# Hybrid decoder trunk: squares of x summed through accumulating transposes, the forget-gate chain on ScalarE, and PE matmuls on a constant at the start

## The reference

```python
h = rmsnorm(x, norm_pre[0])                    # x * rsqrt(mean(x*x) + 1e-6) * g
proj = h @ w_in                                # q | k | v | z | f
log_f = log_sigmoid(proj[..., 4096:] + b_f)    # 16 columns, one per head
c = cumsum(log_f)                              # over the tokens
logit[t, s] = q_t . k_s / 8 + c[t] - c[s]      # causal, then softmax
y = (softmax(logit) @ v) * silu(z) @ w_out
x = x + rmsnorm(y, norm_post[0])
x = x + sigmoid(rmsnorm(x, pe_norm[0]) @ pe_w_gate[0]) * (p[0] @ pe_w_proj[0])
```

## Time and profile before

| | |
|---|---|
| median of three runs | 686.02 us |
| profiled execution | 686.55 us, of which 684.7 us span |
| PE busy | 639.0 us (93%) |
| VectorE, ScalarE, GpSimd busy | 417.5, 340.3, 322.1 us |
| mean granted TensorE clock | 0.992 |
| chain that ended last | PE 60%, DVE 17%, issue 10%, ACT 7%, POOL 4% |

### The profile page before, as it was taken

One profiled execution on the slowest core, in us unless ns is written; L12 is line 12 of the kernel. 1 busy time (PEld: TensorE's weight loads), 2 busy tenths in 40 slices (PEclk: granted clock), 3 DMA queues, 4 the chain that ended last, 5 costly groups with the idle time before them and its releaser, 6 DMA issues.

```text
span 684.7 us, 9410 instructions
## 1 busy us (share of the span) xinstructions
PE 639.0 (93%) x2960; PEld 518.2 (76%) x2960; DVE 417.5 (61%) x797; ACT 340.3 (50%) x582; POOL 322.1 (47%) x416
## 2 busy tenths in 40 slices
PE   4979899999999998999979799999999999999697
PEld 2768778787888876788756578888888888887476
DVE  6657786867868786545768853424333343356865
ACT  7746575655656574365537553223231331555452
POOL 6365455646454565000557727564445642003662
PEclk9999999999999999999999989999999999999999
DMA  6233433333333333044002303332223232350032
GB/s 223 94 104 112 121 129 108 100 102 130 114 108 123 121 100 101 32 161 147 0 32 61 123 32 123 123 99 85 92 92 123 92 123 93 103 174 1 31 100 85
DMA packets 27161, 68.69 MB, mean 100 GB/s; under 512 B 3568, under 2 KB 10096, under 8 KB 27136
## 3 DMA queue, kind: packets, MB, share of 16 engines
q1 hardware_dynamic: 27136, 68.37, 30.6%
HBM read 66.23 MB, written 2.13 MB: 100 GB/s over the span
## 4 chain that ended last, share of the span: by engine, by line
PE 60%; DVE 17%; issue 10%; ACT 7%; POOL 4%; DMA 1%; DVEq 0%; SPq 0%; ACTq 0%; POOLq 0%
PE ps_pj L1079 18%; PE ps_pj L1081 17%; PE ps_pj L1080 17%; POOL w_lo L410 3%; PE ps_tr L1088 2%; DVE q_lo L873 2%; DVE act_lo L970 2%; DVE k_st L881 2%; DVE xT L966 1%; DVE t_a L975 1%; ACT logit L527 1%; ACT k_st L573 1%; DVE logit L817 1%; DVE o_u L829 1%; PE ps_tr L1079 1%
## 5 line engine op out<-in xcount | busy, mean ns | idle before, releaser
L410 POOL TENSOR_TENSOR w_lo<-w_raw,w_hi 128x256 fp32r<-128x256 f32 x324 | 259.8, 834 | 134.1 <-ACT w_hi L474 134.0
L1079 PE MATMUL ps_pj<-act_hi,w_hi 128*128 128x512 f32 (+1 forms) x744 | 298.1, 401 | 17.3 <-DVE act_lo L970 10.6
L1081 PE MATMUL ps_pj<-act_hi,w_lo 128*128 128x512 f32 (+1 forms) x744 | 290.6, 391 | 0.0
L1080 PE MATMUL ps_pj<-act_lo,w_hi 128*128 128x512 f32 (+1 forms) x744 | 290.1, 390 | 0.0
L1079 PEld LDWEIGHTS ps_pj<-act_hi,w_hi 128*128 128x128 f32 x744 | 141.1, 190 | 50.5 <-DVE act_lo L970 14.0
L1081 PEld LDWEIGHTS ps_pj<-act_hi,w_lo 128*128 128x128 f32 x744 | 140.7, 189 | 30.0
L1080 PEld LDWEIGHTS ps_pj<-act_lo,w_hi 128*128 128x128 f32 x744 | 141.2, 190 | 24.9
L474 ACT CAST w_hi<-w_raw 128x1024 fp32r<-128x1024 f32 x96 | 99.8, 1047 | 79.5 <-DMA w_raw<-in_weights 66.7
L418 POOL TENSOR_TENSOR bias<-bias,future 128x128 f32<-128x128 f32 x64 | 33.9, 560 | 88.7 <-DMA bias<-negc_scratch 88.7
L527 ACT ACTIVATE logit<-logit,nmax 128x128 f32<-128x128 f32 (+1 forms) x64 | 36.1, 564 | 61.2 <-DVE nmax L808 61.1
L452 POOL TENSOR_TENSOR t_b<-yT,rs 128x512 f32<-128x512 f32 x4 | 7.1, 1770 | 105.2 <-ACT rs L513 105.2
(11 more groups left out here) (143 smaller groups left out, 780.4 us busy)
## 6 DMA issues: line engine op xcount, KB each, us to landing
w_raw<-in_weights SPq DMA_DIRECT2D x100, 512.0 KB, 3.3
bias<-negc_scratch SPq DMA_DIRECT2D x16, 256.0 KB, 7.5
bias<-negc_scratch SPq DMA_DIRECT2D x16, 192.0 KB, 6.3
xT<-in_xT SPq DMA_DIRECT2D x8, 256.0 KB, 5.7
bias<-negc_scratch SPq DMA_DIRECT2D x16, 128.0 KB, 5.0
out<-xT SPq DMA_DIRECT2D x7, 256.0 KB, 3.3
bias<-negc_scratch SPq DMA_DIRECT2D x16, 64.0 KB, 3.4
p_in<-in_pT SPq DMA_DIRECT2D x2, 512.0 KB, 4.6
```

The lines of the kernel that those rows point to most:

```text
L410: last = nc.gpsimd.tensor_tensor(w_lo[place % RING][:, tiles], w_raw[stream(place) % RAW][:, tiles], w_hi[place % RING][:, tiles], ALU.sub ...
L1079: nc.tensor.matmul(out, w_h, a[0][:, k, tokens], start=k == first, stop=False)
L1080: nc.tensor.matmul(out, w_h, a[1][:, k, tokens], start=False, stop=False)
L1081: end = nc.tensor.matmul(out, w_l, a[0][:, k, tokens], start=False, stop=k == last)
```

## The change

In the first stage, ScalarE squares the even tiles and VectorE the odd ones, into four buffers. PE transposes each square in four pieces of 128 x 128, all eight tiles into one PSUM bank with accumulation (`turn_squares`), so that the bank holds the sums over the eight tiles with tokens on the partitions. One reduction on VectorE gives the sum of squares per token, and ScalarE takes its root with the scale 1/1024. `acc` is not made, and `norm_sum(0)` goes. Slot 0 follows two tiles behind instead of three. `norm_spread(0)` moves from the second to the fifth step of slot 1. Twenty matmuls of a constant with itself, 128 columns each, go ahead of everything else on PE.

In the gate chain, the absolute value with the bias moves to ScalarE, min(x, 0) is made together with the bias on VectorE, and the cumulative sum takes both inputs directly; the constant of ones goes. ScalarE's part stands at g = 1 instead of g = 3, and VectorE's sum stands ahead of `scale(1)`. A table with both Exp and Ln is loaded right after the root. Slot 1 is loaded behind x tile 4 instead of 3, and its high part is copied behind tile 5. The bias buffers move to another place in SBUF.

```diff
+WARM = 20
+SQ_BUFS = 4
+SPREAD_AT = 4
...
-BEHIND = 3
+BEHIND = 2
...
-                if k == 1 or k == 3:
-                    load_slot(k // 2, k // 2)
+                if k == 1 or k == 4:
+                    load_slot(k // 3, k // 3)
...
-            sp.wait_ge(f_chain, 3)
+            sp.wait_ge(f_chain, 1)
...
+            nc.scalar.preload_act_table(ACT.Sqrt)
...
-                wait(act, x_acc, k - 1)
-                nc.scalar.activation(sq[k % 2][:], xT[:, k, :], ACT.Square).then_inc(x_sq, 1)
-                if k % 2 == 1 and k < 4:
-                    weight_hi(k // 2, k // 2)
+                if k % 2 == 0:
+                    wait(act, x_turned, k - SQ_BUFS + 1)
+                    nc.scalar.activation(sq[k % SQ_BUFS][:], xT[:, k, :], ACT.Square).then_inc(x_sq[0], 1)
+                if k == 1 or k == 5:
+                    weight_hi(k // 4, k // 4)
...
-            norm_sum(0)
-
             act.wait_ge(f_done, 1)
             nc.scalar.copy(f_half[:], ps_sc[0][F_PART:F_PART + HEADS, :]).then_inc(f_half_done, 1)
-            norm_root(0)
+            act.wait_ge(ssq_done, 1)
+            nc.scalar.activation(root[:], ssq[:], ACT.Sqrt, bias=EPS, scale=1.0 / D).then_inc(root_done, 1)
+            nc.scalar.preload_act_table_set("natural_log_exp_and_others")
             weight_hi(2, 2)
             norm_spread(0)
...
-                    if not attend and g == 3:
-
-                        act.wait_ge(f_chain, 1)
+                    if not attend and g == 1:
+
+                        act.wait_ge(f_scaled, 1)
+                        act.wait_ge(g_loaded[1], 16)
+                        nc.scalar.activation(f_abs[:], f_x[1][:], ACT.Abs, bias=b_f[:]).then_inc(f_act, 1)
+                        act.wait_ge(f_act, 1)
                         nc.scalar.activation(f_ln[:], f_abs[:], ACT.Exp, scale=-1.0).then_inc(f_act, 1)
-                        act.wait_ge(f_act, 1)
+                        act.wait_ge(f_act, 2)
                         nc.scalar.activation(f_ln[:], f_ln[:], ACT.Ln, bias=1.0).then_inc(f_act, 1)
...
-            nc.vector.memset(ones_f[:], 1.0).then_inc(mean_ready, 1)
...
-                dve.wait_ge(x_sq, k + 1)
-                if k == 0:
-                    nc.vector.tensor_copy(acc[:], sq[0][:]).then_inc(x_acc, 1)
-                else:
-                    dve.wait_ge(x_acc, k)
-                    nc.vector.tensor_tensor(acc[:], acc[:], sq[k % 2][:], ALU.add).then_inc(x_acc, 1)
-
-            def f_parts():
-
-                dve.wait_ge(f_half_done, 1)
-                nc.vector.tensor_tensor(f_x[0][:], ps_sc[0][0:HEADS, :], f_half[:], ALU.add).then_inc(f_self, 1)
-
-            norm(0, f_parts)
+                if k % 2 == 1:
+                    wait(dve, x_turned, k - SQ_BUFS + 1)
+                    nc.vector.tensor_tensor(sq[k % SQ_BUFS][:], xT[:, k, :], xT[:, k, :], ALU.mult
+                                            ).then_inc(x_sq[1], 1)
+
+            dve.wait_ge(f_half_done, 1)
+            nc.vector.tensor_tensor(f_x[0][:], ps_sc[0][0:HEADS, :], f_half[:], ALU.add).then_inc(f_sum, 1)
+
+            dve.wait_ge(x_turned, KT)
+            nc.vector.tensor_reduce(ssq[:], ps_tr[0][:].rearrange("p (t c) -> p t c", c=P), AX.X, ALU.add
+                                    ).then_inc(ssq_done, 1)
+            norm_row(0)
...
             def f_logits():
 
-                dve.wait_ge(f_self, 1)
-                nc.vector.tensor_tensor(f_x[1][:], f_x[0][:], rs[0:HEADS, :], ALU.mult).then_inc(f_self, 1)
+                dve.wait_ge(f_sum, 1)
+                nc.vector.tensor_tensor(f_x[1][:], f_x[0][:], rs[0:HEADS, :], ALU.mult).then_inc(f_scaled, 1)
                 dve.wait_ge(g_loaded[1], 16)
-                dve.wait_ge(f_self, 2)
-                nc.vector.tensor_scalar(f_x[0][:], f_x[1][:], b_f[:], None, ALU.add).then_inc(f_self, 1)
-                dve.wait_ge(f_self, 3)
-                nc.vector.scalar_tensor_tensor(f_abs[:], f_x[0][:], -1.0, f_x[0][:], ALU.mult, ALU.max
-                                               ).then_inc(f_chain, 1)
+                dve.wait_ge(f_scaled, 1)
+                nc.vector.tensor_scalar(f_min[:], f_x[1][:], b_f[:], 0.0, ALU.add, ALU.min).then_inc(f_floor, 1)
 
             def f_sums():
 
-                dve.wait_ge(f_act, 2)
-                nc.vector.scalar_tensor_tensor(f_x[1][:], f_x[0][:], 0.0, f_ln[:], ALU.min, ALU.subtract
-                                               ).then_inc(f_chain, 1)
-                dve.wait_ge(mean_ready, 2)
-                dve.wait_ge(f_chain, 2)
-                nc.vector.tensor_tensor_scan(f_negc[:], ones_f[:], f_x[1][:], 0.0, ALU.mult, ALU.subtract
+                dve.wait_ge(f_floor, 1)
+                dve.wait_ge(f_act, 3)
+                nc.vector.tensor_tensor_scan(f_negc[:], f_ln[:], f_min[:], 0.0, ALU.add, ALU.subtract
                                              ).then_inc(f_chain, 1)
 
             def score_logits(u, m0, jj):
@@ -847,8 +850,8 @@
                         scale(0)
                     if g == 4 and not attend:
                         f_logits()
+                        f_sums()
                         scale(1)
-                        f_sums()
...
+            pe.wait_ge(mean_ready, 1)
+            for _ in range(WARM):
+                nc.tensor.matmul(ps_tr[1][:, 0:P], mean_w[:], mean_w[:], start=True, stop=True)
+
+            def turn_squares(k):
+
+                pe.wait_ge(x_sq[k % 2], k // 2 + 1)
+                for t in range(TT):
+                    tokens = slice(t * P, (t + 1) * P)
+                    last = nc.tensor.matmul(ps_tr[0][:, tokens], sq[k % SQ_BUFS][:, tokens], ident[:],
+                                            start=k == 0 and t == 0, stop=k == KT - 1 and t == TT - 1, is_transpose=True)
+                last.then_inc(x_turned, 1)
+
             pe.wait_ge(f_ready, 1)
             for k in range(KT + BEHIND):
+                if 0 < k <= KT:
+                    turn_squares(k - 1)
...
-                if k == KT + BEHIND - 1:
-                    norm_sum(0)
...
-                if k == 1:
+                if k == SPREAD_AT:
...
-                            pe.wait_ge(f_chain, 1)
+                            pe.wait_ge(f_sum, 1)
```

More of the change, by code:

```diff
@@ L25 @@
 ACT = mybir.ActivationFunctionType
+AX = mybir.AxisListType
 P = 128
@@ L148, in trunk @@
         norms = ExitStack()
-        sq = [sb(f"sq{i}", [P, SEQ], at=norms) for i in range(2)]
+        sq = [sb(f"sq{i}", [P, SEQ], at=norms) for i in range(SQ_BUFS)]
         acc = sb("acc", [P, SEQ], at=norms)
@@ L158, in trunk @@
         f_w = sb("f_w", [P, KT, 2 * F_PART], F32R, f_part)
-        ones_f = sb("ones_f", [HEADS, SEQ], at=f_part)
+        ssq = sb("ssq", [P, TT], at=f_part)
+        f_min = sb("f_min", [HEADS, SEQ], at=f_part)
         f_half = sb("f_half", [HEADS, SEQ], at=f_part)
@@ L194, in trunk @@
         pt_lo = sb("pt_lo", [P, TT * PT_STEP + PT_STEP], F32R, attn)
+        bias = [sb(f"bias{h}", [P, TT, SEQ], at=attn) for h in range(2)]
         o_half = sb("o_half", [P, SEQ], at=attn)
@@ L204, in trunk @@
         k_st = [[sb(f"k_st{b}{h}", [P, SEQ], F32R, attn) for h in range(2)] for b in range(2)]
-        bias = [sb(f"bias{h}", [P, TT, SEQ], at=attn) for h in range(2)]
         attn.close()
@@ L229, in trunk @@
         f_half_done = sem("f_half_done")
-        f_self = sem("f_self")
+        f_sum = sem("f_sum")
+        f_scaled = sem("f_scaled")
+        f_floor = sem("f_floor")
         tr_done = sem("tr_done")
@@ L234, in trunk @@
         mean_ready = sem("mean_ready")
-        x_sq = sem("x_sq")
-        x_acc = sem("x_acc")
+        x_sq = [sem(f"x_sq{i}") for i in range(2)]
+        x_turned = sem("x_turned")
+        ssq_done = sem("ssq_done")
         act_hi_done = sem("act_hi_done")
@@ L489, in _ @@
                                      ).then_inc(act_hi_done, 1)
-                wait(act, x_acc, k - 1)
-                nc.scalar.activation(sq[k % 2][:], xT[:, k, :], ACT.Square).then_inc(x_sq, 1)
-                if k % 2 == 1 and k < 4:
-                    weight_hi(k // 2, k // 2)
-            def norm_sum(n):
-                if n == 0:
-                    act.wait_ge(x_acc, KT)
-                else:
-                    act.wait_ge(acc_done, KT * n)
-                wait(act, st_done, n)
+                if k % 2 == 0:
[3 more added lines that the diff above has]
+                    weight_hi(k // 4, k // 4)
+            def norm_sum(n):
+                act.wait_ge(acc_done, KT * n)
+                wait(act, st_done, n - 1)
                 nc.scalar.copy(acc_hi[:], acc[:]).then_inc(acc_hi_done, 1)
             def norm_root(n):
-                act.wait_ge(st_done, n + 1)
+                act.wait_ge(st_done, n)
                 nc.scalar.activation(root[:], ps_o[:, 0:2 * TT:2], ACT.Sqrt, bias=EPS).then_inc(root_done, 1)
@@ L612, in square @@
                 if n % KT == 0:
-                    act.wait_ge(acc_ready, n // KT + 1)
```

(12 more changed lines are left out.)

## The result

The changed kernel takes 691.84 us, median of 9 runs, against 686.02 for the kernel before: ratio 1.0082, 95% interval 1.0062 to 1.0102, so 0.82% slower. Its profiled execution took 692.13 us with a span of 690.2.

The account below looks back on a forecast made before the run. PE, busy 639.0 of 684.7 us, was taken as the bound, an early score hanging on SP's store of the cumulative sum. 4.4 for the later store plus 0.5 for the clock gave 4.9 us slower: 691.0, range 686.0 to 693.5.

Parts of the forecast that it names:

- The chain: Gate chain delays `w_hi` of slot 3, then SP's load of slot 5, the store and the score: 4.4 us later.
- The clock in the first stage: PE ahead of slot 1: constant matmuls run at the full clock in part, then the clock falls, costing 1.5 us.
- the hole: PE ahead of slot 0, waiting for its `w_lo` until 12.2: over 2 us of nothing at the end.
- I take it that the clock falls again there: PE ahead of slot 0: half speed until near 15.3, costing 1.5 us, so slot 0 ends at 24.1.
- the rival of the kept clock: Constant matmuls hold PE's clock through the first stage: store at 36.7, 3.4 us slower, 689.4; chance 0.22.
- The wait for the store's landing: SP, from the store of the cumulative sum to the bias transfers: 1.6 us, the distance before.
- The clock behind the score: PE behind the late score: the longer wait prolongs the low clock, between nothing and 0.95 more, taken as 0.5.
- the sum of 4.9 us: Whole kernel: 4.4 us for the later store and score plus 0.5 for the clock behind the score.
- the removed loads: ScalarE: two table loads less, each 1.28 us and beside waits, the last Ln's too.
- The load that was added behind the root: ScalarE: puts `w_hi` of slot 2 off to about 25; its `w_lo` ends near 29.4, just ahead of PE's slot 2.
- The rival built on it, 700 us: First stage on PE: clock stays low while transposes stand in each step, chain 9 us further, 700; chance 0.07.

Follow-up runs that it names:

- the chain behind: Changed kernel with ScalarE's part of the gate chain back at g = 3, behind the high part of slot 3: 688.98 us, ratio 1.0024.
- the last run of all three: Changed kernel with chain at g = 3, spread earlier, store and first bias ahead of slot 5, small loads later, and early table load: 686.44 us, ratio 0.9994.

## Why the prediction was right, and where its steps were off

**The chain held, step by step.** `w_hi` of slot 3: forecast 31.3, measured 31.13. Slot 5's load: 36.4, measured 36.09. Store: 38.2, measured 37.89. Slot 6's `w_hi`: 49.7, measured 49.71. Score: 52.9 with a wait of about 6, measured 52.97 with 5.52. All these rows are of an execution that started 0.6 late; from the first `act_lo` on, the store is 3.5 us later than before and the score 3.9, where the forecast had 4.4 for both. The cause is shown, not only argued, from both sides: the kernel before with the chain moved ahead loses 0.95%, the changed kernel with it moved back regains 0.58%. And that the path runs through SP is shown by the store that was put ahead of slot 5: slot 3 stayed late, and 0.55% came back. Some 0.25% is left in both, and not assigned.

**The clock in the first stage was forecast wrong.** The constant matmuls did not bring it up when they ran (20 in 4.53 us, 0.23 each, of a shape that takes half of that at 2.4 GHz), as the forecast had it; the matmuls behind them were still at 1.2 GHz, and the rise came at 11.1, just ahead of the hole. The step "I take it that the clock falls again there" then failed in the profiled execution:

```profile
12.88 0.50 PE L1082 MATMUL ps_pj<-act_hi,w_hi 128*128 128x512 f32 x1 [1.37 <-POOL w_lo L418]
13.21 0.39 PE L1083 MATMUL ps_pj<-act_lo,w_hi 128*128 128x512 f32 x1
13.45 0.39 PE L1084 MATMUL ps_pj<-act_hi,w_lo 128*128 128x512 f32 x1
```

Matmuls stood 0.24 apart behind the hole. The hole itself was mis-sized: the forecast counted PE's work up to it at the full clock and had over 2 us of nothing, but at 1.2 GHz that work took about twice as long, and 1.37 us were left. It is no constant either: with the chain behind, and in another run with only the spread earlier, the rise had not come by the hole, and slot 0 began 0.43 apart. In the last run of all three it had come, the wait was 2.01 us, and the clock fell behind it:

```profile
14.00:16.00 2.00, 2.00 (x9) 0.50 0.83 262
```

In the six other experiments whose slot 0 began at 2.4 GHz, that wait was 1.04 to 1.51 us, and slot 0 went on at 2.4 GHz. In three of them a forget-gate matmul still took 0.63 us just ahead of the wait and 0.39 or 0.40 behind it: there the rise fell into the wait. Other errors made up for most of that term here. The execution started 0.6 late, so that `w_lo` of slot 0 came at 12.9, not 12.2, and slot 0 took 10.7 us from there, where 10.4 were counted at the full clock. So a slow clock that did not come, 1.5 us, stands against 0.9 us of late start and longer stage: slot 0 ended near 23.5, not 24.1, and from there the chain stayed within 0.3 us of its forecast up to the store. That is luck in the size of a term, and by the trace the rival of the kept clock describes the first stage better. Its time, 689.4, does not fit.

**The wait for the store's landing was too short.** From store to bias the forecast took 1.60 us, as before. It took 2.24. In the eight experiments in which the store follows the load of slot 5 within 2 us it took 2.04 to 2.54. Where it stood ahead of that load, in three, it took 1.59 or 1.60, and 1.60 in the kernel before with constant matmuls, where the load is 2.6 ahead. So a late load seems to cost the store twice, in SP's list and then on the way. What holds it on the way is not shown: wherever the load is close, three small loads stand between, the last of them 0.48 us ahead of the store, and no run parts the two. Mask and score came as forecast all the same, since the bias landed 8.35 us behind its issue, not 8.60.

**The clock behind the score: 0.5 was in the sum, and no run shows it.** The low clock lasted longer, as forecast (6 us, before 3.3), but keeping it at 2.4 GHz moved the time by less than can be measured, and left no lead at PE's transposes of v in the next turn. So of the sum of 4.9 us, some 3.9 are seen at the score; the profiled execution is 5.6 us longer, 0.6 of it the late start. That the total came near is in part luck: about 1 us is of a source that the forecast did not have.

**A table load was missed.** The prediction counted the removed loads as covered, and they were. But the last one, before at 46.83 inside ScalarE's wait, is now on the path, at 55.37 between the second logit and Tanh:

```profile
55.37 1.28 ACT L567 ACT_TABLE_LOAD   x1
```

Put back into the wait, it gave nothing that could be measured. The error was in the list; in the sum none shows. The load that was added behind the root was rightly counted as covered here, but it delays `w_hi` of slot 2 once the chain is moved back.

**Transposes and the clock.** The Trainium skill (TensorE: Matmul & The Clock Gate, Part 4: PE-mode transpose) has it that transposes do not count as activity for the clock gate in the usual way. The rival built on it, 700 us, is ruled out: with four transposes in each step the matmuls stayed at the spacing of 2.4 GHz up to the end of slot 0. That is no proof against the rule, since matmuls stand in every step too.

**What stays open.** The median is 5.8 us higher, the score 4.5 later, of which 0.6 is the start of that execution. The shift of PE's transposes of v grows from 5.1 in the turn at 76 us to 5.9 in the turn at 261. Neither the clock nor the table load shows as its cause, though the times could hide 1 us of either; 1 to 2 us are not assigned, nor is why the changed kernel stays 0.24% slower with the chain moved back and 0.27% with the store moved ahead.

## What to carry to other kernels

An engine's list is a queue for everything behind it. Moving a chain "earlier" on ScalarE is only early for its own result; ask which instruction now stands behind it, and follow that one to the queue (here SP's) in which the chain's own result must leave. A result that is ready 5 us before its store can't be helped by being ready sooner: move the store, or what stands ahead of it. And before a low clock or a table load is given a price, look for the wait that comes next: a wait downstream can pay for both.

## What the runs showed of the hardware

- The scan of 16x512 on VectorE took 1.21 us where GpSimd was idle as it started, and 1.76 or 1.77 where GpSimd was at `w_lo` as it started (29.55, with the spread earlier and the chain behind). In the two runs that part the start from the rest, the start decided: with the chain ahead it began `w_lo` 0.21 us into the scan (33.14, 33.35), and the scan took 1.21; with the chain behind it ended `w_lo` some 0.7 us into it (32.52, 33.20), and it took 1.76.
- A small store (32 KB) took 1.59 or 1.60 us from its issue to that of the transfers that wait for it, when the load of 512 KB on the same queue was at least 2.6 us ahead or still to come, and 2.04 to 2.54 when that load was 1.8 us ahead, with three small loads between.
- 20 constant matmuls, 4.53 us of work without a gap, did not bring PE to 2.4 GHz by themselves: the spacing of that level came at 11.1 us in the changed kernel, behind another 4 us of nearly dense matmuls and transposes, and at 19 us in the kernel before with the same 20. The column of the granted clock shows 1.00 from 2 to 12 us of the changed kernel, so at the start of a kernel the level is to be read from the distance of matmuls.
- A switch of the table cost its 1.28 us and no more on ScalarE: `w_hi` starts at 24.64, 0.01 behind the load at 23.35. The Trainium skill (ScalarE: Activation LUTs, What ACT_TABLE_LOAD costs) adds a drain of 1.38 us, which no row of these kernels shows.
